# The opening of a two-block transformer kernel: half of the modulation rows summed on TensorE, and the first weights handed over in two parts

## The reference

```python
mods = (jax.nn.silu(c) @ w_ada[l] + b_ada[l]).reshape(B, N_MOD, D_MODEL)
n = modulate(rmsnorm(h, g_pre[l, 0]), shift(0), scale(0))      # x * (1 + scale) + shift
f = swiglu(n, w_ffn_gate[l, 0], w_ffn_up[l, 0], w_ffn_down[l, 0])
h = h + 0.5 * gate(0) * rmsnorm(f, g_post[l, 0])
```

## Time and profile before

| | us |
|---|---|
| median of 3 runs | 1088.44 |
| lowest, highest | 1088.26, 1089.09 |
| the profiled execution | 1088.02 |
| its span in the profile | 1086.3 |
| TensorE busy | 1057.0 (97%) |
| VectorE busy | 854.4 (79%) |
| ScalarE busy | 549.7 (51%) |

### The profile page before, as it was taken

The page is one execution under the profiler, slowest core; times in us unless marked ns, Lnnn a source line. Parts: engine busy times, 40 slices in busy tenths (PEclk is TensorE's granted clock), DMA queues, the critical chain, the costliest instruction groups (busy, mean ns, idle before and its releaser), DMA issues.

```text
span 1086.3 us, 16196 instructions
## 1 busy us (share of the span) xinstructions
PE 1057.0 (97%) x6136; PEld 924.2 (85%) x6136; DVE 854.4 (79%) x932; ACT 549.7 (51%) x669; POOL 47.6 (4%) x78
## 2 busy tenths in 40 slices
PE   3999999999999999999999999999999999999997
PEld 2999999889988788888978888898887778888886
DVE  6899888678887888887778988877876787666665
ACT  4444343564765754444565444445654456444452
POOL 1000000011120100000010000000100000000001
PEclk9999999999999999999999999999999999999999
DMA  9999997466424598997669999854563536767651
GB/s 340 382 403 389 389 394 265 152 157 218 150 78 155 194 336 309 320 311 239 206 235 350 344 369 339 278 174 136 179 206 104 194 118 226 233 214 231 216 174 59
DMA packets 147140, 265.26 MB, mean 244 GB/s; under 512 B 9769, under 2 KB 104470, under 8 KB 141974
## 3 DMA queue, kind: packets, MB, share of 16 engines
q1 hardware_dynamic: 145376, 261.30, 69.7%
q0 software_dynamic: 1056, 3.17, 1.0%
q10 hardware_dynamic: 662, 0.16, 0.1%
HBM read 263.34 MB, written 1.27 MB: 244 GB/s over the span
## 4 chain that ended last, share of the span: by engine, by line
PE 90%; DVE 4%; ACT 2%; DMA 1%; issue 1%; SPq 1%; POOL 1%; POOLq 0%; DVEq 0%; ACTq 0%
PE ps L1999 18%; PE ps L1930 12%; PE ps L1931 12%; PE ps L1932 12%; PE ps L2005 9%; PE ps L1980 7%; PE ps L1982 6%; PE ps L1983 6%; DMA arena<-in_w_ffn_up 1%; ACT w_hi L838 1%; PE ps L2474 1%; DVE x_res L1405 1%; DVE nT L1251 1%; DVE y_row L1399 0%; PE ps L2293 0%
## 5 line engine op out<-in xcount | busy, mean ns | idle before, releaser
L1228 DVE TENSOR_TENSOR w_lo<-w_raw,w_hi 128x2048 fp32r<-128x2048 f32 (+1 forms) x163 | 367.1, 2254 | 103.3 <-ACT w_hi L838 102.5
L838 ACT ACTIVATE w_hi<-w_raw 128x2048 fp32r<-128x2048 f32 (+2 forms) x169 | 317.5, 1884 | 245.4 <-PE ps L1932 96.4
L1999 PE MATMUL ps<-nT_both,w_hi 128*128 128x512 f32 x864 | 210.7, 391 | 0.0
L1999 PEld LDWEIGHTS ps<-nT_both,w_hi 128*128 128x128 f32 x864 | 158.8, 188 | 30.7
L1980 PE MATMUL ps<-nT_both,w_hi 128*128 128x256 f32 x576 | 164.3, 285 | 0.0
L1982 PE MATMUL ps<-nT_both,w_hi 128*128 128x256 f32 x576 | 162.9, 283 | 0.0
L1983 PE MATMUL ps<-nT_both,w_lo 128*128 128x256 f32 x576 | 162.9, 283 | 0.0
L1320 DVE SCALAR_TENSOR_TENSOR arena<-arena,c_act 128x3072 f32<-128x3072 f32 (+2 forms) x49 | 129.4, 2651 | 0.4 <-DMA arena<-in_ada_w 0.4
L1930 PE MATMUL ps<-w_hi,hT_hi 128*128 128x512 f32 x320 | 125.0, 391 | 0.0
L1931 PE MATMUL ps<-w_lo,hT_hi 128*128 128x512 f32 x320 | 125.0, 390 | 0.0
L1932 PE MATMUL ps<-w_hi,hT_lo 128*128 128x512 f32 x320 | 124.5, 389 | 0.0
(11 more groups left out here) (310 smaller groups left out, 1239.8 us busy)
## 6 DMA issues: line engine op xcount, KB each, us to landing
arena<-in_w_ada SPq DMA_DIRECT2D x16, 1536.0 KB, 9.4
arena<-in_ada_w SPq DMA_DIRECT2D x16, 1536.0 KB, 8.2
w_raw<-in_w_in SPq DMA_DIRECT2D x44, 512.0 KB, 4.5
w_raw<-in_ffn_w_down SPq DMA_DIRECT2D x44, 512.0 KB, 4.1
w_raw<-in_w_ffn_gate SPq DMA_DIRECT2D x42, 512.0 KB, 7.0
w_raw<-in_w_ffn_up SPq DMA_DIRECT2D x42, 512.0 KB, 8.2
w_raw<-in_w_ffn_down SPq DMA_DIRECT2D x42, 512.0 KB, 4.5
w_raw<-in_ffn_w_gate SPq DMA_DIRECT2D x42, 512.0 KB, 4.2
```

Source lines behind the costliest of these rows:

```text
L838: copy = lambda o, i: act.activation(o, i, ACT.Copy)
L1228: dve.tensor_tensor(lo(s, n), raw(s, n), hi(s, n).bitcast(F32), ALU.subtract).then_inc(lo_ready[s], 1)
L1999: pe.matmul(ps[:, i, :], hi(s)[:, cols], nT_both[:, 4 * half + k].rearrange("p a n -> p (a n)"), start=(half == 0 and k == 0), stop=False, ...
```

## The change

- `ON_DVE` is pieces 0 to 3 and `ON_PE` pieces 4 to 7, in both halves. In half 0 TensorE makes 32 one-column products (`first_row(0, j)`) ahead of the first layer, with the fold between pieces 4 and 5, and eight transposes between pieces 6 and 7; in half 1 it makes 24 of them in threes in the second half of (0,1), then the fold, then the last eight. Banks are assigned anew.
- Weights (0,0) and (1,0) are split in two parts of 1024 columns each, on ScalarE and on VectorE, and this now stands behind `first_mods` and in between the normalisation pairs (`first_split`). TensorE starts with tile 0 by pairs: hi x hi and lo x hi of a pair, then hi x lo of all, then tile 1.
- In the opening ScalarE applies scale and shift to tile 0's pairs 0 and 2 only; VectorE does the other six.
- `spin`: 12 products of 128 columns behind the first product and 5 behind `first_mods`, whose results nobody reads.
- SyncE: weights (0,1) are loaded right behind (0,0), the store of `toe_scratch` stands two pieces later, pieces 4 to 7 of half 1 wait for TensorE's row sums of half 0.
- `last_loaded` is merged into `x_loaded`; `trig_ready`, which nothing used, is gone.

```diff
-        ON_DVE = [[0, 1, 2, 3, 4, 5, 6, 7], [0, 1, 4, 5, 6, 7]]
-        ON_PE = [2, 3]
+        ON_DVE = [0, 1, 2, 3]
+        ON_PE = [4, 5, 6, 7]
...
             if f == "F0":
-                return [(t, pair, i) for t, pair in HALF_PAIRS[:6] for i in range(2)]
+                return [(0, pair, i) for pair in (0, 2) for i in range(2)]
...
             load_gu("F0", 0, 0)
+            load_gu("F0", 0, 1)
+            for j in range(2):
+                sp.wait_ge(first_sum, j + 1)
+                load_first(1, j)
             sp.wait_ge(toe_sb, 1)
             sp.dma_start(toe_dram.rearrange("(p n) -> p n", p=P), toe_rows).then_inc(toe_stored, 16)
-            for j in range(KD):
-                sp.wait_ge(first_sum, j + 1)
+            for j in range(2, KD):
+                if j in ON_DVE:
+                    sp.wait_ge(first_sum, j + 1)
+                else:
+                    sp.wait_ge(fold_mm, FOLDS.index("rows 0") + 1)
                 load_first(1, j)
-                if j == 1:
-                    load_gu("F0", 0, 1)
...
-            split_hi(*gate_up("F0", 0, 0))
             for half in range(2):
+                s, use = gate_up("F0", half, 0)
                 act.wait_ge(first_mods, half + 1)
-                for t in range(T):
-                    if half and t:
-                        split_hi(*gate_up("F0", 1, 1))
-                    norm_hi("F0", t, range(2 * half, 2 * half + 2))
-                if half == 0:
-                    split_hi(*gate_up("F0", 0, 1))
-                    split_hi(*gate_up("F0", 1, 0))
+                norm_hi("F0", 0, [2 * half])
+                act.wait_ge(raw_loaded[s], use * 32 + 32)
+                copy(hi(s)[:, 0:D], raw(s)[:, 0:D]).then_inc(first_hi, 1)
+                norm_hi("F0", 0, [2 * half + 1])
+                copy(hi(s)[:, D:PIECE], raw(s)[:, D:PIECE]).then_inc(hi_ready[s], 1)
+                norm_hi("F0", 1, [2 * half, 2 * half + 1])
+                split_hi(*gate_up("F0", half, 1))
...
+            def first_split(half):
+
+                s, use = gate_up("F0", half, 0)
+                a, b = 2 * half, 2 * half + 1
+                dve.wait_ge(first_mods, half + 1)
+                norm_cols("F0", 0, b)
+                norm_cols("F0", 1, a)
+                norm_lo("F0", 0, a)
+                norm_cols("F0", 1, b)
+                dve.wait_ge(first_hi, half + 1)
+                dve.tensor_tensor(lo(s)[:, 0:D], raw(s)[:, 0:D], hi(s)[:, 0:D].bitcast(F32), ALU.subtract).then_inc(first_lo, 1)
+                norm_lo("F0", 0, b)
+                dve.wait_ge(hi_ready[s], use + 1)
+                dve.tensor_tensor(lo(s)[:, D:PIECE], raw(s)[:, D:PIECE], hi(s)[:, D:PIECE].bitcast(F32), ALU.subtract)\
+                    .then_inc(lo_ready[s], 1)
+                norm_lo("F0", 1, a)
+                norm_lo("F0", 1, b)
+                split_lo(*gate_up("F0", half, 1))
...
+            def first_row(half, j):
+
+                pe.wait_ge(first_loaded[j], 16 * (half + 1))
+                for k in range(KD):
+                    last = pe.matmul(ps[:, fold_bank(f"rows {half}"), k:k + 1], first_at[half][j][:, k * P:(k + 1) * P],
+                                     c_act[:, 0, j:j + 1], start=(j == ON_PE[0] and k == 0), stop=(j == ON_PE[-1]),
+                                     skip_group_check=True)
...
                 for half in range(2):
                     s, use = gate_up("F0", half, 0)
-                    weights(s, use)
...
+                    for part in range(2):
+                        pair = 2 * half + part
+                        if part:
+                            pe.wait_ge(hi_ready[s], use + 1)
+                        else:
+                            pe.wait_ge(first_hi, half + 1)
+                        for x, ready in ((nT_hi, n_hi), (nT_lo, n_lo)):
+                            pe.wait_ge(ready, pair_count("F0", 0, pair))
...
+                    row_group(s, o, NB, "F0", 4 * half, start=(half == 0), stop=(half == 1), tiles=(1,)).then_inc(w_used[s], 1)
                     if half == 0:
-                        gate_up_half("F0", 0, 1, each=lambda: next(row_sums, None))
+                        gate_up_half("F0", 0, 1, each=between)
+                        for _ in row_sums:
+                            pass
+                        first_fold(1)
+                        for _ in first_row(1, ON_PE[-1]):
+                            pass
...
+            spin(2, 12)
             pe.wait_ge(small_loaded, SMALL)
...
+            for j in ON_PE:
+                if j == ON_PE[1]:
+                    first_fold(0)
+                if j == ON_PE[-1]:
+                    for t in range(T):
+                        norm_transposes("F0", t, range(2))
+                for _ in first_row(0, j):
+                    pass
             norm_transposes("F0", 0, range(2, PAIRS))
-            first_fold(0)
             pe.wait_ge(vec_ready, 2)
             norm_transposes("F0", 1, range(2, PAIRS))
-            pe.wait_ge(c_ready, 1)
+            pe.wait_ge(first_mods, 1)
+            spin(0, 5)
             ffn("F0")
```

More of the change, by code:

```diff
@@ L281, in program @@
         }
-        FOLDS = ["first 0", "rows 1", "first 1", "F0", "F0 late", "F1", "F2", "F2 late", "F3"]
+        FOLDS = ["first 0", "rows 0", "first 1", "rows 1", "F0", "F0 late", "F1", "F2", "F2 late", "F3"]
         fold_cols = {
@@ L427, in norm_at @@
                 return ps[:, 1, 0:P]
-            at = (2 * (pair % 2) if f == "F0" else 0) + i
+            at = (2 if f == "F0" and (t, pair) in ((1, 0), (0, 2), (1, 3)) else 0) + i
             return ps[:, norm_bank(f, t, pair), at * P:(at + 1) * P]
@@ L2149, in opening @@
-            def opening():
-                o = [ps[:, t, :] for t in range(T)]
-                row_sums = first_row_sums()
+            def first_row(half, j):
[4 more added lines that the diff above has]
+                                     skip_group_check=True)
+                    if k == KD - 1 and j == ON_PE[-1]:
+                        last.then_inc(fold_mm, 1)
+                    yield
@@ L2153, in opening, with between @@
+            def first_row_sums():
+                for j in ON_PE[:-1]:
+                    yield from first_row(1, j)
+            def opening():
+                row_sums, called = first_row_sums(), itertools.count()
+                def between():
+                    if next(called) >= 8:
+                        for _ in range(3):
+                            next(row_sums, None)
                 for half in range(2):
                     s, use = gate_up("F0", half, 0)
-                    weights(s, use)
@@ L2156, in opening @@
-                    for t in range(T):
-                        for k in range(4):
-                            last = row_group(s, o, NB, "F0", 4 * half, start=(half == 0), stop=(half == 1), tiles=(t,), ks=[k])
-                            if half == 0 and t:
-                                if k == 3:
-                                    last.then_inc(w_used[s], 1)
-                                for _ in range(3):
-                                    next(row_sums)
-                        if half and t == 0:
-                            last.then_inc(row_mm, 1)
@@ L2166, in opening @@
-                    if half == 0:
-                        gate_up_half("F0", 0, 1, each=lambda: next(row_sums, None))
-                    else:
-                        last.then_inc(w_used[s], 1)
+                    o = [ps[:, t, :] for t in range(T)]
+                    for part in range(2):
[6 more added lines that the diff above has]
+                            pe.wait_ge(ready, pair_count("F0", 0, pair))
+                            for k in (2 * part, 2 * part + 1):
+                                pe.matmul(o[0], x[:, 4 * half + k, 0:P], hi(s)[:, k * NB:(k + 1) * NB],
+                                          start=(half == 0 and k == 0 and ready is n_hi), stop=False, skip_group_check=True)
@@ new lines, in opening @@
+                    for k in range(4):
+                        if k == 0:
+                            pe.wait_ge(first_lo, half + 1)
+                        if k == 2:
+                            weights(s, use)
+                        last = pe.matmul(o[0], nT_hi[:, 4 * half + k, 0:P], lo(s)[:, k * NB:(k + 1) * NB],
+                                         start=False, stop=(half == 1 and k == 3), skip_group_check=True)
+                    if half:
+                        last.then_inc(row_mm, 1)
@@ L2184, in ffn, with spin @@
                 last_downs(f)
+            def spin(bank, n):
+                for _ in range(n):
+                    pe.matmul(ps[:, bank, 0:P], ident[:], ones[:], start=True, stop=True, skip_group_check=True)
             pe.wait_ge(const_ready, 2)
```

72 lines of the change are left out of this document (22 added, 50 removed).

## The result

The changed kernel takes 1104.54 us (median of 4 runs, 1104.21 to 1105.99) against 1088.35 beside it: a ratio of 1.015, 95% interval 1.0132 to 1.0168. The forecast was 1093.5 with a range to 1099: the sign was right, the size was not. The profiled execution has a span of 1102.5 us, 16.2 more than before.

The account below looks back on a forecast made before the run. TensorE's solid run after its start was taken to bound the kernel. Readiness (0.3 lost), start (1.4 gained), sixteen more products (3.6 lost) and holes (3.1 lost), rounded to 5.0, plus 0.1 for sending, on 1088.4 gave 1093.5 us; range 1091 to 1099.

Parts of the forecast that it names:

- the mark: Start of piece (1,1), last of the four opening pieces: forecast to move from 48.11 to about 53.1 us.
- The price of a product: One-column two-pass product on TensorE: 0.2235 us at 2.4 GHz, up to 0.43 at 1.2 GHz.
- rival 1: Clock falls again during half 0's one-column products: 1096.5 to 1099 us, middle 1098; chance 0.31.
- m: Moment half 0's modulation values are ready on VectorE: forecast 22.6 us, against 22.34 before.
- Rival 2: The twelve filling products don't raise the clock, half 0's products and transposes run at 1.2 GHz: 1102.7 us; chance 0.06.
- Rival 3: Faster: a one-column product costs half; at 0.11 us each the kernel takes 1086.9 us; chance 0.07.
- m to (0,1), 8.6: From half 0's modulation values to the start of the second opening piece: 8.6 us, so it starts at 31.2.
- (0,1) to m2, 13.5: From the second opening piece's start to half 1's modulation values: 13.5 us, so they are ready at 44.7.
- m2 to the mark, 8.6: From half 1's modulation values to piece (1,1): 8.6 us, with 3.1 us of holes on TensorE.
- +1.1: Allowance in the main case's own range, 1091.5 to 1095.5, for a slow second start: 1.1 us.
- DMA: Bytes unchanged; the load waiting for half 1's sums goes at about 44.3 instead of 38.15 and stays hidden.
- The sum: Delay of piece (1,1): 0.3 lost, 1.4 gained at the start, 3.6 and 3.1 lost; written as 5.0 us.

Follow-up runs that it names:

- the kernel with half 0's rows: Kernel before, with only half 0's pieces 4 to 7 moved to TensorE as one-column products, no fillers, half 1 as before: 1095.81 us, ratio 1.0069.
- the dense fillers: Changed kernel with a 128-column filling product ahead of every one-column product, 64 in all: 1109.68 us, ratio 1.0192.
- the variant with fillers at four places: Kernel before, with only 12, 8, 2 and 8 filling products added at four places in TensorE's waits: 1089.43 us, ratio 1.0014.

## Why the prediction was wrong

**What bounds it** was right: the delay of the mark is the delay of the end (16.2 and 16.2; 7.6 and 7.6 in the kernel with half 0's rows).

**The price of a product** was right at either level: 0.22 at 2.4 GHz (row 4; the dense fillers), 0.43 at 1.2 GHz, as the earlier trace rows had suggested. The Trainium skill's price for a load ("TensorE: Matmul & The Clock Gate", section "LDWEIGHTS (loading the stationary operand)"), which names no level of the clock, does not hold at 1.2 GHz: an estimate from that page puts four rows at 6.8 us, where without fillers they take 13.5.

**The step that failed** is the level: "I take 0.2235. That is at 2.4 GHz", carried through both series. The text named the fall as rival 1, but only for half 0, and gave it 0.31. The argument against it, that products of this kind between others had left the clock at 2.4 GHz, came from three of them behind each three 512-column products, and one behind each three of 256. That said nothing of 32 in a row, and nothing of three behind each three of 256 columns in (0,1). Nor did the long series from which the price was taken: its products have 64 columns and keep the pitch of 0.22 for 5.1 us (324.17 to 329.30 in the kernel before), where those with one column lost it in their second row (row 5, 2 to 5 us after their start). The price carried over, the level did not. Row by row, half 0 lost 1.2 in row 5, 1.6 in row 6, 0.85 in the transposes and 1.5 in row 7: the 5.2 us of the table. Half 1 lost 3.2 us in four groups, 0.2 in the fold and 1.6 in row 7: another 5.

**Rival 1** had the clock fall from row 6 on, 4.15 us later for m, or 26.75; it fell in row 5 already, 27.77. So it came to pass, but its sum, 1098, took half 1 at full clock and added 1.3 for transposes and fillers that hold the start back. That 1.3 didn't come (m to (0,1) 8.37; the forecast had 8.6), and half 1's 5.2 and the slow second start were missing: even the rival closest to what happened ended 6.5 us short. Rival 2 is refuted: row 4 ran at 2.4 GHz. Rival 3 as well: the cheapest row cost 0.22 a product.

**m to (0,1), 8.6**: right, 8.37, and 8.45 with half 0 on VectorE. TensorE starts 2.6 us behind m instead of 2.25, since transposes and fillers end only then.

**(0,1) to m2, 13.5**: right as a structure (13.8 with the clock held), short by the clock.

**m2 to the mark, 8.6**: 9.48. The hole is 2.76 us and the start is slow, the "+1.1" that the text had kept for its range. No run of the changed kernel takes the slow start away by itself; its trace bounds it: the split of (1,1) ends at 63.05, and TensorE, busy without a gap since 57.11, is done at 64.30.

**DMA**: the load that waits for half 1's sums was forecast for 44.3, hidden. It went at 54.44, and the queue had run dry by then (158 GB/s from 50 to 60 us in the stretches above):

```profile
54.44 0.34 SPq L592 DMA_DIRECT2D arena<-in_w_ada  x1
```

It cost TensorE nothing: ScalarE's wait for weights, 4.00 us, ends at 82.82 and leaves TensorE without a gap, and from the mark to the end the span is as before. The reason that the text gave, a TensorE late enough, fits this.

**The sum** itself is loose: its terms (0.3, -1.4, 3.6, 3.1) add up to 5.6, the moments to 5.2 (53.3 less 48.11), and the text wrote 5.0. That is small beside the miss.

Together, by the moments: 5.2 us as forecast and 11.0 over it. Of these, 10.4 arose in the two series, where the clock fell; 0.9 arose behind the hole, where the slow start can account for all of it; and 0.2 was gained between m and (0,1).

## What to carry to other kernels

Before work is moved to an idle TensorE, ask at which clock it will run there: long series of products with one column keep the engine busy and let its clock fall, and the large products behind them pay too. Price a long series at the lower level unless a row of equal density shows the upper one. And a start that is earlier by 2 us is worth nothing where the next piece waits for its weights; the pause that it leaves there can cost the clock as well, as it did in some of these runs and not in others.

## What the runs showed of the hardware

- TensorE's clock fell from 2.4 to 1.2 GHz while the engine was busy without a pause: in the second row of eight one-column products (0.22 us each, then 0.43), and in a piece where three of them stand behind each three 256-column products (groups of 1.02 us, then 1.92). In the piece where one stands behind each three it did not fall (groups of 0.58), nor in the series with a 128-column product beside each (0.445 a pair to the end), nor in 5.1 us of products with 64 columns (0.22 each).
- Pauses of 1.52 us (2.7 us at 1.2 GHz behind it) and 1.17 us (eight fillers of 0.42) were followed by the lower clock; in the variant with fillers at four places pauses of 1.97 and 2.45 us were not. The length of the pause alone does not decide it.
- In the kernel before, the granted clock column reads 1.00 even over the stretch in which 512-column products pitch 0.43, and in the run without fillers it reads 1.00 from 13 to 30 us, where the one-column products pitch 0.43. The pitch is the safer witness; after a fall, as above, the column shows it.
